# Two split weight buffers placed elsewhere in SBUF: a three-pass float32r kernel on one core

## The reference, cut to what matters

```python
def swiglu(x, w1, w3, w2):
    return (jax.nn.silu(x @ w1) * (x @ w3)) @ w2
...
    x = layer_norm(DN_ALPHA * x + 0.5 * swiglu(x, ffn1_w1[l], ffn1_w3[l], ffn1_w2[l]), ln1_g[l], ln1_b[l])
    h = split_columns(x @ w_in[l])
...
    return y @ w_out
```

## The kernel before, in words

| tile | before | after |
|---|---|---|
| `xh`, `xl`, `raw`, `ffn_hh`, `ffn_hl`, `ssm_yh`, `lru_h` and their low parts | 0 | 0 |
| `whi` | 0 | 256 |
| `wlo` | 0 | 64 |
| `consts_sb` (identity, masks, rope tables) | 0 | 256 |
| `par` (gains, biases; per-partition scalars) | 32 | 288 |
| `consts_bf` | 32 | 96 |

## Time and profile before

### The profile page before, as it was taken

How to read it: one execution, slowest core, us unless ns; L and a number is a source line. 1 busy time by engine, 2 the same in 40 slices (tenths; PEclk the granted TensorE clock), 3 DMA queues, 4 the chain that set the end, 5 groups by cost and what they waited for, 6 DMA issues and landing times. The chain is left out here.

```text
span 3974.6 us, 44781 instructions
## 1 busy us (share of the span) xinstructions
PE 3586.9 (90%) x16200; PEld 2815.6 (71%) x16200; DVE 1781.4 (45%) x2970; ACT 1450.7 (37%) x2379; POOL 48.9 (1%) x44
## 2 busy tenths in 40 slices
PE   7999989988999899988998899958888897889998
PEld 6887757766888688866667688836766675677886
DVE  3333358444333433344763433355655436534333
ACT  4322425353332432242545332244544325323322
POOL 0000020000000000001000000000000000000000
PEclk9999998788999899999898999979999998899999
DMA  3332310002332233221001233201121121222331
GB/s 135 95 104 76 102 41 1 1 27 69 99 102 89 65 95 104 91 88 55 1 1 38 68 96 104 86 29 49 54 65 54 59 85 61 74 75 85 97 103 65
DMA packets 73728, 276.78 MB, mean 70 GB/s; under 512 B 10368, under 2 KB 11904, under 8 KB 72832
## 3 DMA queue, kind: packets, MB, share of 16 engines
q1 hardware_dynamic: 73600, 275.12, 21.5%
HBM read 272.99 MB, written 2.10 MB: 69 GB/s over the span
## 5 line engine op out<-in xcount | busy, mean ns | idle before, releaser
L344 PE MATMUL ps<-xh,whi 128*128 128x512 f32 x2880 | 1149.6, 399 | 166.5 <-DVE xl L485 70.5
L345 PE MATMUL ps<-xl,whi 128*128 128x512 f32 x2880 | 1134.8, 394 | 0.0
L346 PE MATMUL ps<-xh,wlo 128*128 128x512 f32 x2880 | 1133.6, 394 | 0.0
L316 DVE TENSOR_TENSOR wlo<-raw,whi 128x1024 fp32r<-128x1024 f32 (+2 forms) x464 | 602.3, 1298 | 1062.0 <-ACT whi L312 1061.9
L344 PEld LDWEIGHTS ps<-xh,whi 128*128 128x128 f32 x2880 | 548.9, 191 | 311.5 <-issue 142.2
L312 ACT ACTIVATE whi<-raw 128x1024 fp32r<-128x1024 f32 (+2 forms) x464 | 515.0, 1111 | 496.2 <-PE ps L346 488.4
L346 PEld LDWEIGHTS ps<-xh,wlo 128*128 128x128 f32 x2880 | 549.0, 191 | 116.4
L345 PEld LDWEIGHTS ps<-xl,whi 128*128 128x128 f32 x2880 | 550.3, 191 | 113.2 <-issue 2.4
L344 PE MATMUL ps<-ffn_hh,whi 128*128 128x512 f32 x880 | 345.6, 393 | 12.6 <-DVEq L610 12.6
L346 PE MATMUL ps<-ffn_hh,wlo 128*128 128x512 f32 x880 | 344.7, 392 | 0.0
L345 PE MATMUL ps<-ffn_hl,whi 128*128 128x512 f32 x880 | 344.6, 392 | 0.0
(11 more groups left out here) (327 smaller groups left out, 3936.7 us busy)
## 6 DMA issues: line engine op xcount, KB each, us to landing
raw<-in_ffn_up SPq DMA_DIRECT2D x216, 512.0 KB, 3.5
raw<-in_ffn_down SPq DMA_DIRECT2D x80, 704.0 KB, 4.0
raw<-in_mix_in SPq DMA_DIRECT2D x40, 512.0 KB, 3.5
raw<-in_ssm_in SPq DMA_DIRECT2D x40, 512.0 KB, 3.6
raw<-in_lru_in SPq DMA_DIRECT2D x20, 512.0 KB, 3.7
raw<-in_mix_out SPq DMA_DIRECT2D x16, 512.0 KB, 3.2
raw<-in_ssm_out SPq DMA_DIRECT2D x12, 512.0 KB, 3.6
raw<-in_lru_out SPq DMA_DIRECT2D x8, 640.0 KB, 3.9
```

What stands on the lines that cost most here:

```text
L316: dve.tensor_tensor(self.core.wlo[:, u % HALF, 0:width], self.core.raw[:, u, 0:width], self.core.whi[:, u % HALF, 0:width].bitcast(F32), A ...
L344: pe.matmul(out, c.whi[:, h, w], xh[:, k0 + k], start=first and k == 0, stop=False)
L345: pe.matmul(out, c.whi[:, h, w], xl[:, k0 + k], start=False, stop=False)
L346: mm = pe.matmul(out, c.wlo[:, h, w], xh[:, k0 + k], start=False, stop=last and k == nk - 1)
```

## The change

The low buffer comes first now, 64 bytes further than before modulo 512; the high buffer follows with a gap of 192 bytes, which puts it at 256. All that lies behind them moves up by 256 bytes. The parameter tile, of which at most 75 columns are used, shrinks from 128 to 80 columns, which gives 192 bytes back, so that the end of the used range is 64 bytes higher. No instruction is added, removed or moved: on each engine the list is the same, and only addresses differ.

```diff
-A_WHI = A_RAW + RAW * SLOT * 4
-A_WLO = A_WHI + HALF * SLOT * 4
-A_CONST = A_WLO + HALF * SLOT * 4
+A_WLO = A_RAW + RAW * SLOT * 4 + 64
+A_WHI = A_WLO + HALF * SLOT * 4 + 192
+A_CONST = A_WHI + HALF * SLOT * 4
...
-A_KB = A_PAR + 128 * 4
+A_KB = A_PAR + 80 * 4
...
-        self.par = self.at("par", [P, P], F32, A_PAR)
+        self.par = self.at("par", [P, 80], F32, A_PAR)
```

## The result

The changed kernel is slower: 4022.92 us (median of 4 runs, 3998.63 to 4028.43) against 3941.12 us in the same comparison, a ratio of 1.0197 with a 95% interval of 1.0154 to 1.0239. The profiled execution has a span of 4026.6 us, 52.0 us more than before.

The account below looks back on a forecast made before the run. PE was taken as the bound, through the start-to-start distance of float32r matmuls. The terms, -61 us for the buffer positions and 0 for all else, gave 3942.65 - 61 = 3882 us, with 8 in 10 between 3820 and 3982.

Parts of the forecast that it names:

- What bounds the kernel: PE, busy 90%; 11904 matmuls on lines 344 to 346 at 226.8 ns start to start, 68% of the span.
- the ring: The float32r matmuls on lines 344 to 346, 226.8 ns apart at full clock, 13.4 ns over the columns alone.
- The price, 11.1 us for each ns: 1 ns on each of 11904 matmuls is 11.9 us, of which 0.93 was said to reach the end.
- Half of what could be gained, 5.5 ns, 61 us: Lines 344 to 346: new buffer positions make each matmul 5.5 ns shorter, saving 61 us.
- The bound of the possible gain: At best float32r matmuls reach bf16's distance, about 215.6 ns: 11.2 ns less each, 124 us.
- The high buffer at 256 as half a period: Half a period of distance for the load of `whi`, which occurs twice in three, as the plainest way to avoid collisions.
- The stream leaves no free turn for the 512 bytes: Float32r at full clock: the 13.4 ns excess looks like an SBUF read limit, with weights read beside the stream.
- Rival B: New positions are worse ones: +3.6 ns a matmul gives 3983 us, at 240 ns 4090; chance 0.24.
- the worst bound of 147 us: Lines 344 to 346 at 240 ns, as in a group with 64-partition operands: 13.2 ns more each.
- What would show it: Over 443 matmuls in the third FFN window, 452 at 221 ns; distances might differ between lines 344 to 346.
- ACT, DVE, constants, parameter tile at 0 us: Splits on lines 312 and 316 keep 1051 and 1225 ns; moved constants and smaller parameter tile cost 0 us.
- The Trainium skill's two ports: Two independent SBUF read ports on TensorE; by that rule the place of `whi` and `wlo` is worth 0 us.

Follow-up runs that it names:

- experiment 6: Both split buffers at 64, constants at 256, otherwise the kernel before: ratio 1.0200 (1.0152 to 1.0248), 700.0 ns a triple.
- experiments 1 to 3: Against the kernel before: probe map of operand positions (680.0 ns a triple lowest); both split buffers at 256 (ratio 1.0001); only the high buffer and constants at 256 (1.0018).
- experiment 5: Kernel before plus a second probe stretch, second stream moved, other shapes and formats, 15 matmuls a case: bf16 216 ns, unsplit float32 429 ns from record to record.
- experiment 9: Probes of experiment 5 with 36 matmuls a case, 256 arrangements: only the kernel before's has 680.0 ns a triple; the next 686.5 to 686.8, the highest 710.
- experiment 3: Only the high buffer and constants at 256, low buffer at 0, otherwise the kernel before: ratio 1.0018 (0.9978 to 1.0058), 680.6 ns a triple.
- experiment 4: Low buffer at 64, high buffer first at 0, constants at 256, otherwise the kernel before: ratio 1.0129 (1.0052 to 1.0205), 693.3 ns a triple.
- experiment 8: Only constants and parameters move by 256, parameter tile shrinks, both split buffers at 0, otherwise the kernel before: ratio 0.9990 (0.9954 to 1.0025).

## Why the prediction was wrong

- **What bounds the kernel: right.** PE's start-to-start distance in the ring makes 47 of the 52 us between the spans by the price, and no other engine's work moved; the other 5 us are not traced.
- **The price, 11.1 us for each ns: right,** 11.3 in experiment 6.
- **"Half of what could be gained, 5.5 ns, 61 us": the step that failed, by its sign.** In place of a gain of 5.5 ns the change cost 4.24 ns a matmul, some 50 us. Behind it stood the thought that two streams which start at the same position get in each other's way, so that any distance between them helps. The maps show the reverse: the common position is the one arrangement of 256 in which the distance is lowest, and none of them gains anything over it. The bound of the possible gain, bf16's 215.6 ns, wasn't within reach of any arrangement tried.
- **The high buffer at 256 as half a period: wrong.** The period is 256 and not 512 (experiments 1 to 3), so this part of the change did nothing, and the weight of two loads in three that I gave it was a weight on nothing.
- **"The stream leaves no free turn for the 512 bytes": not borne out.** Its signs were right as far as they went: at the low clock, with bf16 and with unsplit float32 the excess is 0 to 3 ns and doesn't depend on place (bf16 and unsplit float32 in experiments 5 and 9, for the stationary block alone). But a block of a quarter of the columns has no smaller excess, so it doesn't follow the bytes loaded. What exacts it, and whether the load has a part in it at all, stays open; a matmul whose weights aren't loaded beside the one ahead of it wasn't tried.
- **Rival B had the outcome, and one of its two reasons.** Position 0 has the lowest distance found anywhere, and that was B's second reason. Its first, that the load of `whi` meets the stream in a worse phase, was wrong: `whi` at 256 changed nothing (experiment 3), and the loss came with `wlo` at 64 (experiment 4), to which B had given the smaller weight. Its price, 3.6 ns, was near the 4.24 measured, and its time of 3983 us is 1.0% above the kernel before, where 1.2 to 1.3% is what the change costs. The price was the mean of lines 724 to 726 at other positions, so that it came this near is in part luck. The evidence for B stood in the rows: no group under 13 ns in the earlier trace rows. I named it and then gave a general idea of how collisions work more weight than eight measured positions.
- **Three readings of rows were off,** none of which turns the sum. The five of the earlier trace rows are records, and an unsplit float32 matmul leaves two (experiment 5), so it runs at a quarter of the speed and not at half; per record there is still hardly an excess. The 240 ns of the earlier trace rows, on which the worst bound of 147 us stood, are the longest of 21 such distances in the same trace, 229 to 240 ns. And by the records the triples of the earlier trace rows take 630 to 645 ns, an excess of 15 to 20 ns and not up to 22.
- **What would show it:** the three lines do part (228.4, 229.3, 235.6 ns). I had called that the plainest proof that the load is what the stream meets. It isn't: after lines 344 and 346 the load beside the matmul is of the same buffer, and they part most.
- **ACT, DVE, constants, parameter tile at 0 us: right** (rows above, experiment 8).
- **The Trainium skill's two ports** (page "TensorE: Matmul & The Clock Gate", section "Step-by-step: what each phase is for"), by which a weight load takes no read bandwidth from the running matmul, were read as making place worth nothing. The trace doesn't agree with that reading for float32r at full clock: 680.0 to 710 ns a triple by place alone. Whether the load is what the stream meets there, no run shows. It agrees for bf16 and unsplit float32, 216 and 429 ns with the stationary block at four places.

## What to carry to other kernels

Here, triples of float32r matmuls at full clock, with streams of 512 columns and blocks of 128, depend on where their operands stand modulo 256 bytes, by up to 4% between one arrangement and another. For this shape, keep streams and stationary blocks on the same position, on multiples of 32 bytes, and don't let a small tile ahead of them push them off it. For other shapes the good place may be another, as experiment 9 shows, and has to be measured. Before moving a buffer, look at what the present place costs above the columns; if no group in the trace shows less, as here, take seriously that the place may be the good one already. A probe ahead of the kernel's own work maps hundreds of arrangements in one run. Give it at least 36 matmuls a case, reach the promising ones from more than one starting point, and test the choice in the kernel.

## What was not expected

The pace is a rhythm of several matmuls. In experiment 9 most cases settle within ten matmuls, some take up to 20, and a few repeat no pattern of up to twelve matmuls within their 36. Most of the values lie in steps of 6.67 ns a triple, with a period of 256 bytes and a window of 16 bytes on either side of the good place (680.0 at h = l = 240, 0 and 16, 700.0 at 32). And two executions of one kernel can differ by some 30 us by the clock granted in the attention, 0.80 or 0.91 in the window above, which is more than half of this change's effect: for an effect of 1% the distances in the trace say more than the medians of four runs.
